# The score products of the gates stage as split fp32r products, set among the first chunk's matmuls

## What is computed

```
z      = einsum('bqhd,bshd->bhqs', q, k) * scale          # stick-breaking branch
a      = where(mask, exp(log_sigmoid(z) + suffix), 0)     # suffix: reverse sum of log(1 - beta)
o_sb   = einsum('bhqs,bshd->bqhd', a, v)

logits = einsum('bqhd,bqkhd->bhqk', q, k_sel) * scale     # indexed sparse branch
p      = softmax(where(valid, logits, -inf))
o_ds   = einsum('bhqk,bqkhd->bqhd', p, v_sel)

merged = sigmoid(g_sb) * (o_sb @ w_branch[:SB_W]) + sigmoid(g_ds) * (o_ds @ w_branch[SB_W:])
```

## Time and profile before

| | us |
|---|---|
| median of 3 runs | 1435.22 |
| lowest and highest | 1435.05 and 1436.7 |
| the profiled execution | 1435.36 |
| its span, first to last instruction | 1433.5 |
| PE busy | 1428.1 |
| DVE busy | 1140.3 |
| ACT busy | 841.6 |
| POOL busy | 447.8 |

### The profile page before, as it was taken

One profiled execution on the slowest core, in us unless ns is written; L12 is line 12 of the kernel. 1 busy time (PEld: TensorE's weight loads), 2 busy tenths in 40 slices (PEclk: granted clock), 3 DMA queues, 4 the chain that ended last, 5 costly groups with the idle time before them and its releaser, 6 DMA issues.

```text
span 1433.5 us, 23730 instructions
## 1 busy us (share of the span) xinstructions
PE 1428.1 (100%) x7626; PEld 1223.7 (85%) x7626; DVE 1140.3 (80%) x1533; ACT 841.6 (59%) x1181; POOL 447.8 (31%) x493
## 2 busy tenths in 40 slices
PE   9999999999999999999999999999999999999999
PEld 7888888888888888888888888888888888888887
DVE  6778998886656566899967778777778778999998
ACT  7545667666767666666664455455554545465553
POOL 2310000333132213650025455655556555200000
PEclk9999999999999999999999999999999999999999
DMA  8665665665555555567666666666666665576664
GB/s 255 191 196 173 210 194 183 197 176 176 161 162 158 168 171 178 188 222 233 191 178 182 186 199 182 186 191 190 191 191 180 185 195 189 192 230 206 202 209 147
DMA packets 121064, 272.26 MB, mean 190 GB/s; under 512 B 10688, under 2 KB 10976, under 8 KB 121008
## 3 DMA queue, kind: packets, MB, share of 16 engines
q1 hardware_dynamic: 119936, 268.99, 60.7%
q0 software_dynamic: 896, 2.42, 0.6%
q10 hardware_dynamic: 176, 0.14, 0.0%
HBM read 269.42 MB, written 2.10 MB: 189 GB/s over the span
## 4 chain that ended last, share of the span: by engine, by line
PE 98%; DVE 1%; DMA 0%; issue 0%; ACT 0%; SPq 0%; DVEq 0%; ACTq 0%
PE bank L2086 97%; DVE lo L1215 0%; DMA raw<-in_w_in 0%; PE bank L2140 0%; PE bank L2359 0%; PE bank L2400 0%; DVE y L1758 0%; PE bank L2223 0%; DVE msum L1234 0%; ACT hi L720 0%; SPq L550 0%; DVE msum L1243 0%; DVE msum L1240 0%; DVE lo L1098 0%; ACT hi L637 0%
## 5 line engine op out<-in xcount | busy, mean ns | idle before, releaser
L1098 DVE TENSOR_TENSOR lo<-raw,hi 128x1024 fp32r<-128x1024 f32 (+1 forms) x342 | 444.3, 1304 | 167.1 <-ACT hi L637 166.5
L637 ACT ACTIVATE hi<-raw 128x1024 fp32r<-128x1024 f32 (+1 forms) x342 | 359.2, 1053 | 272.0 <-PE bank L2086 263.8
L2086 PE MATMUL bank<-h2T,hi 128*128 128x512 f32 x1408 | 483.3, 394 | 0.0
L2086 PE MATMUL bank<-h2T,lo 128*128 128x256 f32 x1408 | 376.8, 278 | 0.0
L2086 PEld LDWEIGHTS bank<-h2T,hi 128*128 128x128 f32 x1408 | 257.9, 188 | 53.5
L2086 PE MATMUL bank<-hT,hi 128*128 128x512 f32 (+1 forms) x784 | 272.8, 394 | 0.1
L2086 PEld LDWEIGHTS bank<-h2T,lo 128*128 128x128 f32 x1408 | 264.5, 188 | 7.8
L2086 PE MATMUL bank<-hT,lo 128*128 128x256 f32 (+1 forms) x784 | 212.6, 281 | 0.0
L2050 POOL TENSOR_TENSOR u<-u,rms_row 128x256 f32<-128x256 f32 x88 | 120.8, 1373 | 184.8 <-DVE u L1610 165.8
L2086 PE MATMUL bank<-hi,ffT 128*128 128x512 f32 x576 | 177.3, 389 | 0.0
L2086 PEld LDWEIGHTS bank<-hT,hi 128*128 128x128 f32 (+1 forms) x784 | 143.9, 187 | 29.7 <-DVE lo L1098 0.3
(11 more groups left out here) (298 smaller groups left out, 2023.8 us busy)
## 6 DMA issues: line engine op xcount, KB each, us to landing
raw<-in_w_up SPq DMA_DIRECT2D x176, 512.0 KB, 3.9
raw<-in_w_in SPq DMA_DIRECT2D x160, 512.0 KB, 3.7
raw<-in_w_down SPq DMA_DIRECT2D x88, 512.0 KB, 4.5
raw<-in_w_branch SPq DMA_DIRECT2D x32, 512.0 KB, 3.6
raw<-in_w_out SPq DMA_DIRECT2D x24, 512.0 KB, 5.0
raw4h<-in_w_in SPq DMA_DIRECT2D x8, 512.0 KB, 3.6
raw5h<-in_w_in SPq DMA_DIRECT2D x8, 512.0 KB, 4.0
y<-in_x SPq DMA_DIRECT2D x4, 512.0 KB, 6.5
```

The lines of the kernel that those rows point to most:

```text
L637: act.activation(hi[s][:, 0:width], raw[s][:, 0:width], ACT.Copy)\
L1098: dve.tensor_tensor(lo[s][:, 0:width], raw[s][:, 0:width], hi[s][:, 0:width].bitcast(f32), ALU.subtract)\
L2086: return pe.matmul(o, l, r, start=start, stop=stop, skip_group_check=True)
```

## The change

The three staged operands become one tile `qk_raw` with four parts (z's q and k, the logits' k and q). DVE splits it for the next head into `qk_hi` and `qk_lo` (`qk_split`: a copy of 128 x 1024 numbers and a subtraction of the same size) at j = 4 of each turn, behind `lo` of chunk 7; for the first head it does so ahead of the loop. On PE each plain fp32 product becomes three fp32r products, hi by hi, lo by hi and hi by lo. They are issued as six parts of two products (256 and 128 columns), through the new argument `between` of `cols_chunk`: one part behind each of the first six steps of chunk 0, instead of a block behind the chunk. POOL's `stage_ds` moves ahead of the mask of `stick`.

```
--- before.py
+++ after.py
@@ -245,9 +245,9 @@
 
         W0 = A0 + 7 * KB
         part = [at(f"part{i}", [S], W0 + i * KB) for i in range(4)]
-        sb_q = at("sb_q", [S], W0 + 4 * KB)
-        sb_k = at("sb_k", [S], W0 + 5 * KB)
-        ds_qk = at("ds_qk", [2 * S], W0 + 6 * KB)
+        qk_raw = at("qk_raw", [4, S], W0 + 4 * KB)
+        qk_hi = at("qk_hi", [4, S], 44 * KB, f32r)
+        qk_lo = at("qk_lo", [4, S], 48 * KB, f32r)
         sb_v = at("sb_v", [TH, HD], W0 + 8 * KB)
         ds_v = at("ds_v", [TH, HD], W0 + 9 * KB)
         partb = [at(f"partb{i}", [S], W0 + (4 + i) * KB) for i in range(4)]
@@ -441,6 +441,8 @@
         bpart_done = sem("bpart_done")
         bcol_done = sem("bcol_done")
         staged_qk = sem("staged_qk")
+        qk_hi_done = sem("qk_hi_done")
+        qk_lo_done = sem("qk_lo_done")
         staged_v = sem("staged_v")
         z_full = sem("z_full")
         logit_full = sem("logit_full")
@@ -1468,9 +1470,19 @@
             dve.tensor_scalar(bias[:, :], scores[:, :], (NONCAUSAL + TAKEN) / 2, MASKED,
                               ALU.is_gt, ALU.mult).then_inc(bias_raw, 1)
 
-            def gates_body(h):
+            def qk_split(h):
+
+                dve.wait_ge(staged_qk, 3 * h + 3)
+                dve.tensor_copy(qk_hi[:, :, :], qk_raw[:, :, :]).then_inc(qk_hi_done, 1)
+                dve.wait_ge(qk_hi_done, h + 1)
+                dve.tensor_tensor(qk_lo[:, :, :], qk_raw[:, :, :], qk_hi[:, :, :].bitcast(f32),
+                                  ALU.subtract).then_inc(qk_lo_done, 1)
+
+            def gates_body(h, more):
                 for j in range(CPG):
                     split(C_GATES + AHEAD + j, h, CPG // SLOTS)
+                    if j == 4 and more:
+                        qk_split(h + 1)
                     if j == 1:
 
                         dve.wait_ge(logit_full, h + 1)
@@ -1505,8 +1517,10 @@
                                       oT[:, ds(at_head, 1), 0:S].bitcast(f32), ALU.subtract)\
                         .then_inc(done, 1)
 
-            with dve.Fori(0, NH) as h:
-                gates_body(h)
+            qk_split(0)
+            with dve.Fori(0, NH - 1) as h:
+                gates_body(h, True)
+            gates_body(NH - 1, False)
 
             def merged_lo(n, ct):
                 dve.wait_ge(mT_hi, 4 * n + ct + 1)
@@ -1949,15 +1963,15 @@
 
             def stage_sb(h):
 
-                pool.tensor_tensor(sb_k[:, :].unsqueeze(1), qkT[:, ds(h, 1), S:2 * S],
+                pool.tensor_tensor(qk_raw[:, 1:2, :], qkT[:, ds(h, 1), S:2 * S],
                                    sb_scale[:, :].unsqueeze(1).to_broadcast([P, 1, S]),
                                    ALU.mult).then_inc(staged_qk, 1)
-                pool.tensor_copy(sb_q[:, :].unsqueeze(1), qkT[:, ds(h, 1), 0:S])\
+                pool.tensor_copy(qk_raw[:, 0:1, :], qkT[:, ds(h, 1), 0:S])\
                     .then_inc(staged_qk, 1)
 
             def stage_ds(h):
-                pool.tensor_copy(ds_qk[:, :].unsqueeze(1), qkT[:, ds(NH + h, 1), :])\
-                    .then_inc(staged_qk, 1)
+                pool.tensor_copy(qk_raw[:, 2:4, :].rearrange("p (n a) s -> p n (a s)", n=1),
+                                 qkT[:, ds(NH + h, 1), :]).then_inc(staged_qk, 1)
 
             with pool.Fori(0, 3) as i:
                 gains_body(i)
@@ -1991,12 +2005,11 @@
 
                     pool.wait_ge(logit_full, h + 1)
                     stage_sb(h + 1)
+                    stage_ds(h + 1)
                 wait_alone(pool, stick_raw, h + 1)
                 pool.affine_select(out=diagonal(stick), in_=diagonal(stick), compare_op=ALU.is_gt,
                                    fill=0.0, base=0, pattern=[[0, 2], [1, P]],
                                    channel_multiplier=-1).then_inc(stick_done, 1)
-                if more:
-                    stage_ds(h + 1)
 
             pool.wait_ge(col_scaled, 4)
             pool.wait_ge(qkT_done, 8)
@@ -2110,7 +2123,7 @@
                         i.then_inc(full, 1)
                 i.then_inc(w_used, 1)
 
-            def cols_chunk(c, slot, src, kts, bank, first, last, free, full):
+            def cols_chunk(c, slot, src, kts, bank, first, last, free, full, between=None):
 
                 wh = hi[slot][:, :].rearrange("p (k c) -> p k c", k=CK)
                 wl = lo[slot][:, :].rearrange("p (k c) -> p k c", k=CK)
@@ -2126,9 +2139,14 @@
                                last and j == CK - 1)
                         if first and j == 0:
                             mm(bank[ct][:, 0:S], wl[:, j, cs], src[:, kt, 0:S], False, False)
+                        if between is not None and j == 0:
+                            between(2 * ct)
                     if last and ct < 3:
                         i.then_inc(full, 1)
-                i.then_inc(w_used, 1)
+                    if ct == 3:
+                        i.then_inc(w_used, 1)
+                    if between is not None:
+                        between(2 * ct + 1)
 
             def transposes(k, kts, src, bank=B):
 
@@ -2365,25 +2383,40 @@
             with pe.Fori(1, 4) as i:
                 heads_body(i)
 
+            def split_product(out_, left, right, part, first):
+
+                (l_hi, l_lo), (r_hi, r_lo) = left, right
+                return mm(out_, l_lo if part == 1 else l_hi, r_lo if part == 2 else r_hi,
+                          first and part == 0, part == 2)
+
+            def qk(n, cols):
+                return qk_hi[:, n, cols], qk_lo[:, n, cols]
+
+            def scores_part(h, k):
+
+                old, new, every = slice(0, P), slice(P, S), slice(0, S)
+                if k == 0:
+                    pe.wait_ge(qk_lo_done, h + 1)
+                    pe.wait_ge(qkT_done, 8)
+                if k < 3:
+                    split_product(B[0][:, 0:S], qk(1, old), qk(0, every), k, True)
+                    i = split_product(B[0][:, S:KEYS], qk(1, new), qk(0, new), k, False)
+                    if k == 2:
+                        i.then_inc(z_full, 1)
+                elif k < 6:
+                    split_product(B[1][:, 0:P], qk(2, old), qk(3, old), k - 3, True)
+                    i = split_product(B[1][:, P:KEYS], qk(2, new), qk(3, every), k - 3, False)
+                    if k == 5:
+                        i.then_inc(logit_full, 1)
+
             with pe.Fori(0, NH) as h:
                 def free_gate(ct):
                     pe.wait_ge(col_done, 16 + 4 * h - 4 + ct + 1)
                 for j in range(CPG):
                     cols_chunk(C_GATES + CPG * h + j + 1, j % SLOTS, hT,
                                range(CK * j, CK * (j + 1)), A, j == 0, j == CPG - 1,
-                               free_gate, col_full)
-                    if j == 0:
-
-                        pe.wait_ge(staged_qk, 3 * h + 3)
-
-                        pe.wait_ge(qkT_done, 8)
-                        mm(B[0][:, 0:S], sb_k[:, 0:P], sb_q[:, :], True, True)
-
-                        mm(B[0][:, S:KEYS], sb_k[:, P:S], sb_q[:, P:S], False, True)\
-                            .then_inc(z_full, 1)
-                        mm(B[1][:, 0:P], ds_qk[:, 0:P], ds_qk[:, S:S + P], True, True)
-                        mm(B[1][:, P:KEYS], ds_qk[:, P:S], ds_qk[:, S:2 * S], True, True)\
-                            .then_inc(logit_full, 1)
+                               free_gate, col_full,
+                               (lambda k: scores_part(h, k)) if j == 0 else None)
                     if j == 4:
                         pe.wait_ge(neg_set, 2)
                         pe.wait_ge(stay_lo_done, h + 1)
```

## The result

The changed kernel takes 1450.17 us (median of 5 runs, 1448.0 to 1451.73) where the kernel before takes 1435.22: a ratio of 1.01, with a 95% interval of 1.0089 to 1.0112. That is 15.0 us or 1% slower, 8.3 us more than I forecast and 4.7 beyond the upper end of the range. The profiled execution took 1448.0 us, its span is 1446.1: 12.6 us more than before.

What follows compares the result with a forecast made beforehand. PE was taken as the bound, so its work and waits count: 1435.36 - 2.2 (PE's own work) + 3.5 (first head) + 5.2 (waits for `prob`) = 1441.9 us, 0.45% slower; 8-in-10 range 1435.8 to 1445.5.

Steps and rivals of the forecast that it cites:

- The first head's wait: Start of the gates stage: PE waits 3.4 to 4.1 us for DVE's split, taken as 3.5, with nothing hiding it.
- The wait for `prob`: Ahead of the transposes in every head: PE waits 0.45 to 1.0 us for POOL's scaling, taken as 0.65; chance 0.52.
- What is hidden: The next head's split on DVE delays `lo` of chunks 8 and 9, but 4 us of cover remain for PE.
- PE's own work: Scores on PE: fp32 block of 1.32 us replaced by six parts of 1.04; gain 0.28 us a head, 2.2 in eight.
- My rival of that name: Short products cost 0.12 us, not 0.058: 3.0 us more; with `prob` waits shrinking as much, sum near 1442; chance 0.06.
- the sign of a missed wait: A gates-stage turn over 26.6 us, or `qk_lo` late in a later head, would show a wait was missed.
- the pace of 0.347: PE's steps within the chunks: 0.347 us each for 256 + 512 columns, read from the trace before the change.
- a rival at 0.07: The first head's pause drops PE's clock to 1.2 GHz, adding 2.8 to 5.6 us: 1444.7 to 1447.5; chance 0.07.

Runs made afterwards that it cites:

- e3: The changed kernel with one more wait on DVE: `lo` of chunk 7 starts only when POOL has scaled `prob`; 1443.0 us, ratio 1.0056.
- e1: The changed kernel with the six split parts as one block behind chunk 0 instead of singly inside it; 1439.69 us, ratio 1.0032.
- e6: The changed kernel with nothing split: four plain fp32 products, singly behind the first four steps of chunk 0; 1444.44 us, ratio 1.0062.
- e5: The changed kernel with the split made but not used; PE makes four plain fp32 products behind chunk 0; 1435.3 us, ratio 0.9998.
- e7: e1 with its six short 128-column products left out, so the output is not the reference's; one execution, 1434.11 us.
- e4: The changed kernel with z's three short products widened from 128 to 256 columns, the extra ones unread; 1449.43 us, ratio 1.0096.
- e0: The changed kernel run again, unaltered; 1450.33 us, ratio 1.0101.
- e2: The changed kernel with the first head's scores as plain fp32 products behind its chunk 0, no split made for it; 1444.33 us, ratio 1.0059.
- e9: e10 with only the 256-column products split; the 128-column ones stay plain fp32, one of them last in the block; 1434.41 us, ratio 0.999.
- e10: e1 with the first head in plain fp32 as in e2; 1437.33 us, ratio 1.0011.
- e11: e9 with the two plain 128-column products moved ahead of the split ones in the block; 1435.89 us, ratio 1.0.
- e8: e1 with one fp32 transpose of the identity added behind the block; 1440.79 us, ratio 1.0032.

## Why the prediction was wrong, by its own steps

Right were the direction and the two largest terms. *The first head's wait*: 3.5 forecast, 3.4 us in the profile. *The wait for `prob`*: 0.65 forecast, 0.66 measured, by the mechanism forecast: in place of it e3 takes `lo` out of POOL's way and the wait is gone, e1 puts the scores back and it is gone, e6 has it without a split. *What is hidden*: nothing lost, e5.

The step that failed is **PE's own work**, the choice of 0.058 us for a short product. I took it from 397.01 to 397.07 in the earlier trace rows, the distance from the first short suffix product to the next start. That distance holds half the price. The other half falls on the product behind, whose successor's load cannot come sooner: 397.07 to 397.19, 0.12 us, which I set aside as an upper bound. It is the same in chunk 0 of the change, where the short products themselves take 0.06 and the products behind them 0.06 more than usual, whether they have 256 columns or 512. A 256-column product takes 0.12 and covers its own load, no more; every short product pays its load in full. e7 and e4 show it: 0.113, and columns free up to 256. So a head gains -0.09 instead of 0.28, in eight heads 3.0 us.

My rival of that name said that with waits for `prob` the dearer parts would be given back, so that the sum stays near 1442. That was wrong too. The chain that ends in `prob` starts at PE itself, with `w_used` of chunk 0: `hi` of chunk 4 on ACT comes 4.48 us into the turn (391.15), where I had 4.13, and these 0.35 us are the parts' extra cost. `prob` came as much later as PE did, and the wait stayed as it was. (A turn of 26.73 us is over the 26.6 that I named as the sign of a missed wait. No wait was missed; the excess is these dearer parts and the slow steps.)

Two terms were missing from the sum. *The slow steps*: 0.2 us in each of eight turns and 1.3 in the branch stage, 3.0 us; I had taken the pace of 0.347 as given. *The clock*: I left its fall to a rival at 0.07 because before showed no pause of that length; it fell in three of the four profiled executions that have the pause, for 2.9 us in e0, the lower end of the rival's 2.8 to 5.6, and for 1.6 in e4. At the full clock the sum closes: 1441.9 + 3.0 + 3.0 = 1447.9 against the 1448.0 of the profiled execution. The median is 2.2 above that. This last figure is a remainder and not measured by itself: the clock's fall is of its size, but executions also differ by 1.5 us ahead of the gates stage (e0, e2), and how much of that is in the median no trace shows.

What stays open is why the pace has two values. It isn't the clock (1.00 in both), the split's work (e5), fp32r in the scores or the short products (e6, e7). In the gates stage the steps were fast in every turn in which a plain fp32 product was the last thing ahead of chunk 1 (before, e5, e9, and the first turns of e2, e10 and e11) and slow in nearly all others. The exceptions are the first turn of e1 and the second of e8, both fast, so this is a pattern and not a rule; e9 against e11 shows only that the order matters. For the branch stage I have no rule: it was slow in the profiled executions of the change, e2, e4, e6, e7 and e8, fast in those of e1, e3, e5, e9, e10 and e11, and e8 differs from e1 by one transpose. Whether one kernel can have either pace there from one execution to the next is open; e1's seven slower executions would fit it.

## What to carry to other kernels

Price a short fp32r product by the spacing of weight loads (0.11 us here), and read a price from a stretch that holds the product behind it too, since the distance to the next start showed only half; three cheap products are no bargain at 128 columns. Before you put work among the first steps of a chunk, follow the semaphore at the chunk's end: whatever PE does ahead of it comes back as a delay of the whole chain that starts there, and a shift of half a microsecond on DVE can lengthen what POOL does beside it by one. The late chain alone (e3) and the longer scaling alone (e7) cost PE no wait here; together they made it. A pause of 3 us on TensorE is to be priced with a fall of the clock behind it, not only with its length.

## What the runs showed of the hardware

- A pause of 3.2 us on PE was followed by a granted clock of 0.50 for some 6.8 us in the profiled execution of e0, for about half of that in those of e3 and e4, and by no fall in the change's own. It cost 2.9 us in e0, nearly as much as the pause, and 1.6 in e4.
- Weight loads of 128 x 128 fp32r tiles follow each other no closer than 0.11 us. The Trainium skill (TensorE: Matmul & The Clock Gate, section LDWEIGHTS) gives 128 columns over 1.2, some 107 ns, and the trace agrees. (The first two loads of the `prob` transposes, 403.45 and 403.51 in the change, are 0.06 apart.) The same page (section Back-to-back issue gap) has about 81 ns as the sustained spacing of 128-column products; the six here cost 113 ns each, and the measurement decides.
- The same stream of products runs at 0.347 or 0.353 us a step at the full clock, for tens of microseconds on end, with nothing between the two. Which one it is can hang on the order of eight products ahead of it (e9, e11), but the same order ran at both in two heads of e8.
